# Decode ticks moved from prompt attention into the projection units, and prompt attention in a new order, in a one-core decoder step

## What is computed

```
def fox_attend(q, k, v, cq, ck, q_pos, k_pos):       # 16 heads of 64
    s = einsum('bqhd,bkhd->bhqk', q, k) * 64**-0.5
    s = s + (cq[..., :, None] - ck[..., None, :])    # sums of log forget values
    s = where(k_pos[None, :] <= q_pos[:, None], s, min)
    p = softmax(s, axis=-1)
    return einsum('bhqk,bkhd->bqhd', p, v)

k, v, fl = split(rms_norm(x, kv_norm) @ kv_w)        # k: rms_norm per head
q, z     = split(rms_norm(x, b_norm) @ w_q)          # q: rms_norm per head
out = (attend(q) * silu(z)) @ w_out
```

## Time and profile before

| | |
|---|---|
| median of 3 runs | 2476.58 us (2471.9 to 2484.28) |
| profiled execution | 2480.89 us, its span 2479.0 us |
| TensorE matmul busy | 2227.3 us (90%) |
| VectorE, ScalarE, GpSimd busy | 1314.7 us (53%), 951.9 us (38%), 1072.3 us (43%) |
| mean granted TensorE clock | 0.957 |
| DMA | 430.97 MB, mean 174 GB/s |
| projection units | 1076 to 1632 us |
| prompt attention | 1632 to 2253 us |

### The profile page before, as it was taken

One profiled execution on the slowest core, in us unless ns is written; L12 is line 12 of the kernel. 1 busy time (PEld: TensorE's weight loads), 2 busy tenths in 40 slices (PEclk: granted clock), 3 DMA queues, 4 the chain that ended last, 5 costly groups with the idle time before them and its releaser, 6 DMA issues.

```text
span 2479.0 us, 47140 instructions
## 1 busy us (share of the span) xinstructions
PE 2227.3 (90%) x16540; PEld 1916.8 (77%) x16540; DVE 1314.7 (53%) x1892; ACT 951.9 (38%) x1617; POOL 1072.3 (43%) x715
## 2 busy tenths in 40 slices
PE   5999999999349998979999999979888888988999
PEld 3999999999138998969999787745555555558998
DVE  4689888988791016565776211124544544434332
ACT  4556556655451013222222122324444444443121
POOL 0698899889673213443334333222222222211231
PEclk7999999999789999989999999989998999988999
DMA  3222222222133121132322778999999999963112
GB/s 112 65 70 75 80 67 69 74 75 71 37 122 122 46 77 59 64 133 98 123 80 94 265 263 324 346 349 398 388 381 375 389 368 356 388 252 107 52 59 83
DMA packets 137488, 430.97 MB, mean 174 GB/s; under 512 B 23889, under 2 KB 40658, under 8 KB 136162
## 3 DMA queue, kind: packets, MB, share of 16 engines
q1 hardware_dynamic: 121554, 375.94, 41.4%
q0 software_dynamic: 13168, 41.58, 4.7%
q10 hardware_dynamic: 2592, 11.14, 1.1%
HBM read 386.81 MB, written 43.87 MB: 174 GB/s over the span
## 4 chain that ended last, share of the span: by engine, by line
PE 57%; POOL 15%; DVE 11%; issue 8%; ACT 6%; DMA 2%; ACTq 0%; SPq 0%; POOLq 0%; DVEq 0%
POOL ACC L1346 7%; PE PS L602 6%; PE PS L600 6%; PE PS L601 6%; PE PS L698 5%; PE PS L700 5%; PE PS L699 5%; PE PS L765 4%; PE PS L821 4%; PE PS L874 3%; PE PS L901 3%; PE PS L889 2%; POOL ML L1376 2%; PE PS L608 2%; POOL WL L1319 2%
## 5 line engine op out<-in xcount | busy, mean ns | idle before, releaser
L1319 POOL TENSOR_TENSOR WL<-RAW,WH 128x1024 fp32r<-128x1024 f32 (+1 forms) x121 | 306.2, 2531 | 603.7 <-ACT WH L954 598.6
L1658 DVE SCALAR_TENSOR_TENSOR PS<-UX,CWT,PS 128x1024 f32<-128x1024 f32 (+1 forms) x672 | 466.3, 784 | 0.0
L633 PE MATMUL PS<-HH,WH 128*128 128x384 f32 (+1 forms) x1152 | 378.5, 329 | 20.7 <-DVE HL L1644 20.7
L635 PE MATMUL PS<-HH,WL 128*128 128x384 f32 (+1 forms) x1152 | 377.4, 328 | 0.0
L634 PE MATMUL PS<-HL,WH 128*128 128x384 f32 (+1 forms) x1152 | 377.2, 327 | 0.0
L1346 POOL TENSOR_TENSOR ACC<-ACC,PROD 128x1088 f32<-128x1088 f32 x112 | 284.9, 2544 | 31.4 <-ACT PROD L1006 25.2
L698 PE MATMUL PS<-GH,WH 128*128 128x384 f32 (+1 forms) x792 | 271.0, 342 | 25.5 <-DVE KC L1770 12.1
L700 PE MATMUL PS<-GH,WL 128*128 128x384 f32 (+1 forms) x792 | 262.8, 332 | 0.0
L699 PE MATMUL PS<-GL,WH 128*128 128x384 f32 (+1 forms) x792 | 261.7, 330 | 0.0
L633 PEld LDWEIGHTS PS<-HH,WH 128*128 128x128 f32 x1152 | 217.3, 189 | 24.7 <-issue 13.7
L954 ACT ACTIVATE WH<-RAW 128x1024 fp32r<-128x1024 f32 (+1 forms) x121 | 131.4, 1087 | 253.4 <-PE PS L602 218.0
(11 more groups left out here) (213 smaller groups left out, 4348.2 us busy)
## 6 DMA issues: line engine op xcount, KB each, us to landing
KV<-ck SPq DMA_DIRECT2D x256, 512.0 KB, 7.7
KV<-cv SPq DMA_DIRECT2D x256, 512.0 KB, 7.2
RAW<-wA SPq DMA_DIRECT2D x48, 512.0 KB, 3.3
RAW<-wP SPq DMA_DIRECT2D x16, 640.0 KB, 3.9
zT_scr<-ZS ACTq DMA_DIRECT2D x16, 544.0 KB, 2.7
Z<-zT_scr SPq DMA_DIRECT2D x16, 544.0 KB, 3.6
RAW<-wB SPq DMA_DIRECT2D x17, 512.0 KB, 3.3
RAW<-wO SPq DMA_DIRECT2D x16, 512.0 KB, 3.3
```

The lines of the kernel that those rows point to most:

```text
L633: pe.matmul(out, WH[w][:, kk], HH[:, k, a:b], start=k == 0, stop=False)
L635: mm = pe.matmul(out, WL[w][:, kk], HH[:, k, a:b], start=False, stop=k == KD - 1)
L1319: pool.tensor_tensor(WL[s][:, 0:n], RAW[s][:, 0:n], WH[s][:, 0:n].bitcast(F32), ALU.subtract).then_inc(s_lo, 1)
L1658: i = dve.scalar_tensor_tensor(out=o, in0=x, scalar=w[:, j:j + 1], in1=o, op0=ALU.mult, op1=ALU.add)
```

## The change

1. The queries' units come before the keys'. The ticks need only queries and old pages at first, so `tick_after` now places ticks from the third K unit on: UNIT_TICKS gives 15 in K units, 41 in V and 64 in Z, 120 in all, up to one after each k group. The ring of four slots now lasts for 108 half-steps.
2. For that the per-head norm is done in place in banks 0 to 2 (NCHAIN): one root over 1088 columns on ScalarE, reciprocal and product from there on VectorE, RS3 is gone, and TensorE's norm matmul waits for the norm before (s_kn) and no longer only for its root. KN's store is issued by ScalarE in `sample_columns`, and raw weights of K units by GpSimd. The first sample's new keys come at tick 15, their PV as a step of its own (`first_new`) at tick 68, with tiles PTN0, OE0, OT0, RID0.
3. Prompt attention runs over items: scores of item q, then transposes of item q - 1, then its PV, with three places for ticks between. VectorE takes both maxima of an item before it normalises. Transposes use bank 5 and, for items with over four key blocks, bank 1 or 3 (`t_bank`), which the item in work leaves free; bank 6 is left to decode.

```diff
-U_CONV, U_OUT, U_PLE, U_F, U_K, U_Q, U_V, U_Z, U_W, U_TAIL = 0, 48, 64, 72, 73, 81, 89, 97, 105, 113
+U_CONV, U_OUT, U_PLE, U_F, U_Q, U_K, U_V, U_Z, U_W, U_TAIL = 0, 48, 64, 72, 73, 81, 89, 97, 105, 113
...
+        NCHAIN = PS[:, 0:3, :].rearrange("p a n -> p (a n)")[:, 0:R]
...
+        UNIT_TICKS = (0, 0, 2, 2, 2, 3, 3, 3) + (0, 1, 6, 6, 7, 7, 7, 7) + (8,) * PAIRS
+        SPOTS = {0: (), 1: (7,), 2: (3, 7), 3: (2, 5, 7), 4: (1, 3, 5, 7), 5: (1, 3, 4, 6, 7), 6: (1, 2, 3, 5, 6, 7),
+                 7: (1, 2, 3, 4, 5, 6, 7), 8: (0, 1, 2, 3, 4, 5, 6, 7)}
...
+        for q in range(N_ITEMS):
+            due = T_UNITS + T_LEAD + -(-(q + 1) * (T_END - T_UNITS - T_LEAD) // (N_ITEMS - 1))
+            n = min(due, T_END) - done
+            cuts = {0: (0, 0, 0), 1: (0, 1, 1), 2: (0, 1, 2), 3: (1, 2, 3), 4: (1, 2 + done % 2, 4)}[n]
+            ticks_of.append([range(done + a, done + e) for a, e in zip((0,) + cuts, cuts)])
             done += n
...
+        def t_bank(x, c):
+
+            if order[x % 16 // 2] < 4:
+                return 5
+            return ((5, 1), (3, 5))[x % 2][c]
...
                 pe.wait_ge(s_sq3, p + 1)
-                atleast(pe, s_rs, p)
-                colsum(pe, 0, SQ3, w=BONES).then_inc(s_n, 1)
+                atleast(pe, s_kn, p)
+                for a, b in ((0, 512), (512, 1024), (1024, R)):
+                    mm = pe.matmul(NCHAIN[:, a:b], BONES, SQ3[:, a:b], start=True, stop=True)
+                mm.then_inc(s_n, 1)
...
+            for q in range(N_ITEMS):
+                scores(q // NQ, q % NQ)
+                ticks_and_sides(ticks_of[q][0])
+                if q > 0:
+                    prompt_transpose(2 * q - 2)
+                ticks_and_sides(ticks_of[q][1])
+                if q > 0:
+                    prompt_transpose(2 * q - 1)
+                ticks_and_sides(ticks_of[q][2])
+                if q > 0:
+                    prompt_pv((q - 1) // NQ, (q - 1) % NQ)
...
                 act.wait_ge(s_kn, p + 1)
-                if p == PAIRS:
+                act.dma_start(qT[p] if p < PAIRS else kT[p - PAIRS], KN[:]).then_inc(s_kst, 16)
+                if p == 0:
                     act.wait_ge(s_pad2, 1)
...
+            for q in range(N_ITEMS):
+                for hl in range(2):
+                    for i in ticks_of[q][hl]:
+                        decode_tick(i)
+                    prompt_exp(2 * q + hl)
+                    if q > 0:
+                        prompt_evac(2 * q - 2 + hl)
+                for i in ticks_of[q][2]:
+                    decode_tick(i)
...
+            pool.wait_ge(s_os, 1)
             load_keys(0)
...
+            for q in range(N_ITEMS):
+                prompt_max(2 * q)
+                prompt_max(2 * q + 1)
+                for hl in range(2):
+                    for i in ticks_of[q][hl]:
+                        decode_tick(i)
+                    prompt_probs(2 * q + hl)
+                for i in ticks_of[q][2]:
+                    decode_tick(i)
+                if q > 0:
+                    prompt_o((q - 1) // NQ, (q - 1) % NQ)
```

More of the change, by code:

```diff
@@ new lines, in tick_after @@
+        def tick_after(u, k):
+            if u < U_K:
+                return None
+            spots = SPOTS[UNIT_TICKS[u - U_K]]
+            return sum(UNIT_TICKS[:u - U_K]) + spots.index(k) if k in spots else None
+        NEW_AT = (15,) + (1,) * (DB - 1)
+        I_FIRST = T_B + 32
+        T_UNITS, T_LEAD, T_END = sum(UNIT_TICKS), 4, T_B * DB + 4
+        H_UNITS = sum(i % T_B < 16 or 18 <= i % T_B < 34 for i in range(T_UNITS)) // 4 * 4
+        N_ITEMS, N_STEPS = NQ * PAIRS, 16 * DB
+        N_SLOTS = 2 * N_ITEMS
@@ L829, in decode_pv, with first_new @@
                 mm.then_inc(s_dd, 1)
+            def first_new():
+                pe.wait_ge(s_vr, PAIRS)
+                pe.wait_ge(s_dv, 18)
+                for y in range(4):
+                    mm = pe.matmul(PS[32 * y:32 * y + 32, 6, 0:4 * HD], PTN0[:, 32 * y:32 * y + 32],
+                                   VNW[:, 4 * HD * y:4 * HD * y + 4 * HD], start=True, stop=True)
+                mm.then_inc(s_fn, 1)
             pe.wait_ge(s_t2, KD)
@@ L908, in _, with ticks_and_sides @@
             pe.wait_ge(s_zx, PAIRS)
[L909 to L929, removed]
+            def ticks_and_sides(spot):
+                for i in spot:
+                    decode_tick(i)
+                    decode_side(i, 0)
+            for q in range(N_ITEMS):
[9 more added lines that the diff above has]
+                    prompt_pv((q - 1) // NQ, (q - 1) % NQ)
+            prompt_transpose(N_SLOTS - 2)
+            prompt_transpose(N_SLOTS - 1)
             prompt_pv(PAIRS - 1, NQ - 1)
@@ L1140, in norm @@
                 atleast(act, s_kn, p)
[L1142 to L1145, removed]
+                scale, eps = (1.0, C_EPQ) if p < PAIRS else (1.0 / HD, C_EPS)
+                g = act.activation(NCHAIN, NCHAIN, ACT.Sqrt, scale=scale, bias=CST[:, eps:eps + 1])
                 g.then_inc(s_rs, 1)
@@ L1222, in forget_exp, with ticks @@
                 act.activation(FC_E[:], FC_E[:], ACT.Exp).then_inc(s_fe, 1)
+            def ticks(u):
+                for k in range(KD):
+                    i = tick_after(u, k)
+                    if i is not None:
+                        decode_tick(i)
             for p in range(2 * PAIRS):
-                weights_hi(U_K + p + 1)
+                weights_hi(U_Q + p + 1)
+                ticks(U_Q + p)
                 if p >= 2:
@@ L1242, in _ @@
                     norm(2 * PAIRS - 1)
[L1243 to L1246, removed]
+                ticks(u)
             silu(PAIRS - 1)
@@ L1506, in _ @@
             for p in range(2 * PAIRS):
[L1507 removed]
+                weights(U_Q + p)
                 if p == 0:
@@ L1931, in _ @@
                 u = U_V + m
-                for k in range(KD):
-                    i = tick_after(u, k)
-                    if i is not None:
-                        decode_tick(i)
+                ticks(u)
                 if m < PAIRS:
```

248 lines of the change are left out of this document (115 added, 133 removed).

## The result

The changed kernel takes 2499.6 us (median of 5, 2499.4 to 2509.5); the kernel before, run beside it, 2479.9. The ratio of the runs is 1.011 (95% interval 1.009 to 1.013; the two medians alone are 20 us or 0.8% apart). So it is about 1% slower, where 0.7% faster was forecast.

The account below looks back on a forecast made before the run. TensorE was taken as the bound, transfers second. Units +70 us and attention -87 (work -52, waits -25, clock -10) gave -17 us: 2460 us against a median of 2476.6, 0.7% faster, range 2440 to 2482.

Parts of the forecast that it names:

- Units, +70 us: Projection units: 44 more half-steps, unit ends, row maxima with new scores, and Z-unit transfer waits add 70 us.
- Work, -52: Attention stage: 44 half-steps and the new keys leaving it save 52 us of TensorE's time.
- The waits that go: Attention stage: L808, L776 and L791 lose 21.5 us, L889 13.4, L800 falls from 16.2 to 10.8, the start loses 4.
- The waits that come: Attention stage: next scores (L865) and PV wait 35 us for ScalarE, in place of 15.5.
- uncut 59 us: Attention stage: PV's waits for ScalarE over 64 items by the prediction's arithmetic, before the factor 0.59 made them 35 us.
- Pages: Transfer waits: 6 us in the Z units; at the attention stage's start 4 of 15.1 us go.
- The clock: Attention stage: loss from half clock falls in proportion to waits, from 33 to 23 us; bounds 10 and 35.
- D: Attention stage: order changes but gaps do not shrink, waits and clock as before; +18 us, 2495 us; chance 0.10.
- A: Attention stage: ScalarE's chain becomes the bound and the full 59 us appear; +16 us, 2493 us; chance 0.16.
- B: Z units: bound by transfers at 335 GB/s, 21 us of waits in place of 6; 2475 us; chance 0.18.
- C: Attention stage: ScalarE's chain stays hidden (15.5 us), clock loses 10; -50 us, 2427 us; chance 0.18.
- The signs that the prediction named for itself: Wrong if L865 and PV hold over 50 or under 20 us, Z-unit pages over 15, or clock stays 0.92.

Follow-up runs that it names:

- e2: The changed kernel with 72 ticks in the units in place of 120: 2463.4 us.
- e3: The changed kernel with the second head's transposes of items of 1 to 3 key blocks in bank 7 in place of bank 5: 2499.0 us.
- e5: The changed kernel with ScalarE's second copy of the item before ahead of the second exponential of the current item: 2475.8 us.
- e8: The changed kernel, still 120 ticks, with ScalarE's second copy first, small items' second transposes in bank 7 and SP's weight loads late: 2452.8 us.
- e6: The changed kernel with 72 ticks in the units and ScalarE's second copy ahead of the second exponential: 2445.2 us.
- e7: As e6, and with the small items' second transposes in bank 7: 2442.4 us.
- e9: As e6, but with 96 ticks in the units (none in K units): 2467.6 us.
- e12: As e7, with SP's weight loads at half-step 248 and V units' ticks behind groups 0, 2, 4, 6: 2437.7 us.
- the three edits: ScalarE's second copy ahead of the second exponential, small items' second transposes in bank 7, SP's late weight loads; with 120 ticks 2452.8 us.

## Why the prediction was wrong

**Units, +70 us: right.** 67 to 70 in every pair of profiles with 72 and 120 ticks. By kinds, against the earlier trace rows and their like, K units +21 (forecast 24), V +15 (17), Z +31 (28 with the transfers). But inside the Z units the parts are others: pages, given 6 us, hold 1.2, and one wait of a sample's new part (L798) for decode's exponential, which has the row maximum before it, takes 5.3. All further row maxima and new scores had been given 1 us:

```profile
1610.59 0.48 PE L798 MATMUL PS<-FCON,SC 128*128 128x128 f32 x1 [5.34 <-ACT SC L1219]
```

That the sum came out is luck in this part.

**Work, -52: right like with like.** 507 to 457 from e2 to the changed kernel, 50 us. Against the kernel before it is 44, since the new order itself adds 6 to this sum, which I had not counted.

**The waits that go: right.** L808's and its like's, 21.5 us, are down to 1.0, L889's 13.4 for the probabilities are gone, L800's fell to 4.4 (forecast 10.8), with 5 more than before in the units, as just said.

**The waits that come: here the prediction failed.** "What is late next is ScalarE" was the right place, and of the 35 us given to scores and PV, PV took 31.7; the scores' wait for the exponential does not appear in the list at all. But that step counted the copies only as what PV waits for. The transposes of the second head wait for the copy of the first, since small items have one bank for both and large ones share bank 5 between the first head's and the second head's chunks; the line of the diff that waits for `evacs(x - 1, 0)` was in front of me and was put at nothing. It measured 29.8 us. With it the sum of waits is 61 + 30 = 91 us, and TensorE was idle for 94. An estimate of the whole sum is then +18 us with the 28 us of clock loss that were measured, +25 with a loss in proportion to the waits; the medians are 20 us apart. Smaller misses nearly cancel in this: work and pages cost more than forecast, L800 less.

The two waits are linked, but not one: e3 took 19 us from the transposes and gave 7 to PV, and the time stayed, while e5 took 23 from PV, left the transposes' 30 as they were, and gained 24. Once the copy stood first, the transposes' wait counted too: from e5 to e8 it fell from 30.0 to 10.9 us and pages from 16.6 to 9.4, and the median fell by 23. With 72 ticks (e6 to e7) it fell by 14 and the median by only 2.7. So the 29.8 us belong in the sum of waits, but what they cost by themselves is not shown. That the uncut 59 us of my own arithmetic are near the 61.5 of both lines together proves nothing, since that arithmetic had no such wait in it. The factor of 0.59 came from an order with another chain (probabilities between two maxima); for PV alone its 35 came out near 31.7, and nothing here shows why it should.

**Pages.** I looked for them in the Z units, where TensorE waits 1.2 us (forecast 6), and at the start of the stage, where it waits 9.0 for pages and 0.6 for queries (forecast 11). The 8.3 us at the stage's end come from an order on SP's queue that the move shifted against the items. That queue I had not followed past the tick count.

**The clock.** The forecast took the loss in proportion to the waits, 38% of them, 23 us. In the runs it goes with idle time only roughly: 94 us idle with a loss of 28, 73 with 20, 64 to 65 with 16 to 17, but in e9 64 with 24, in e8 55 with 20, and in e12 64 with 13. That is 21 to 37%.

Of the rivals, D is the nearest in its sum, +18 us: idle time and clock loss together are 122 us after and 119 before, and new waits stand in the old ones' place, though not for the reason given there. A comes near in time (2493 us), but not by its condition: L865 and the PV line were to hold over 47 us and hold 31.7. B's pages did not come in the Z units (1.2 us), and C's hidden chain (15.5 us) did not come in the changed kernel. It came in e7, where PV, transposes and scores together wait 15.2 us for ScalarE, with 72 ticks and 2442.4 us. The signs that the prediction named for itself did not catch the failure either: these two lines lie between 20 and 50 us, and pages below 15. A sign was missing for waits on lines that the sum put at nothing.

The move of the ticks, for which I had worked out a loss of 18 us by itself, did lose: 10 us with the three edits, 31 with the copy first, 36 with neither.

## What to carry to other kernels

When work that fills gaps is moved to a stage that has none, it pays its price there in full and saves less where it was, since the gaps remain: count the cover it gave, not only its busy time. When a chain is pipelined by one item, walk each engine's queue once in order and ask of each instruction who wants it first; here one copy behind one exponential cost 24 us. And for every copy, list all that waits for it: not only who reads what it wrote, but also who wants the bank that it empties.

## What the runs showed that was not expected

With the copy first, 48 and 96 ticks are 27 and 22 us slower than 72, so a split of work can be steep on both sides of its best. Once ScalarE's order was mended, idle time of 64 us was left in both e7 and e9 though one has 24 ticks fewer to cover with.

The granted clock before the units, which no kernel of this study touches, is 0.91 or 0.92 in six of the thirteen profiles and 0.95 in the other seven (650 to 1078 us: 353 us busy in the changed kernel, 344 in the kernel before). The first scaling comes at 1116.6 us in the changed kernel and at 1111.2 in e2, so this is worth up to 5 us of a span. Differences of spans smaller than that are not read from single profiles here; the medians decide.
